# Two channel blocks taken last in the projection, and the modulation's strips multiplied by twos

## What is computed

```python
sh, sc, gt = adaln(c, w_ada, b_ada)              # silu(c) @ w_ada + b_ada, in three parts
sh_c, sc_c, gt_c = adaln(c_ctx[None], w_ada, b_ada)
h_l = rmsnorm(x_l, norm_g) * (1.0 + sc) + sh     # 512 x 2048
h_c = rmsnorm(x_c, norm_g) * (1.0 + sc_c) + sh_c # 256 x 2048
u_l = h_l @ w_in                                  # 2048 x 4928
u_c = h_c @ w_in[:, OFF_KV:OFF_MLA_G]
```

## Time and profile before

| what | value |
|---|---|
| median of 3 runs | 901.35 us |
| profiled execution | 901.99 us |
| its span | 900.2 us |
| mean granted TensorE clock | 0.997 |
| phase A on TensorE ends, phase B begins | 126.7 us |
| TensorE busy | 886.3 us, 98% |
| DMA | 184 MB, of it some 45 MB in the first 112 us |

### The profile page before, as it was taken

How to read it: one execution, slowest core, us unless ns; L and a number is a source line. 1 busy time by engine, 2 the same in 40 slices (tenths; PEclk the granted TensorE clock), 3 DMA queues, 4 the chain that set the end, 5 groups by cost and what they waited for, 6 DMA issues and landing times.

```text
span 900.2 us, 12252 instructions
## 1 busy us (share of the span) xinstructions
PE 886.3 (98%) x4750; PEld 739.2 (82%) x4750; DVE 696.5 (77%) x860; ACT 426.2 (47%) x633; POOL 200.0 (22%) x167
## 2 busy tenths in 40 slices
PE   9999999999999999999999999999999999999996
PEld 5776688888888888888888888989898988888885
DVE  5555898789997699967787484778687787879796
ACT  4655467434335434333324332645454456645464
POOL 1222200310003100001002753100000200495641
PEclk9999999999999999999999999999999999999998
DMA  9999932235473453578874242865657535875754
GB/s 362 417 420 421 409 145 95 89 129 189 143 183 106 114 167 117 187 232 325 314 295 162 94 140 94 181 228 141 135 171 198 123 140 187 305 228 187 234 186 187
DMA packets 36885, 184.08 MB, mean 204 GB/s; under 512 B 4411, under 2 KB 5819, under 8 KB 26716
## 3 DMA queue, kind: packets, MB, share of 16 engines
q1 hardware_dynamic: 32528, 147.25, 44.4%
q0 software_dynamic: 3968, 35.65, 16.2%
q10 hardware_dynamic: 332, 0.40, 0.1%
HBM read 177.39 MB, written 37.75 MB: 239 GB/s over the span
## 4 chain that ended last, share of the span: by engine, by line
PE 90%; DMA 4%; DVE 3%; ACT 2%; issue 1%; SPq 0%; ACTq 0%; DVEq 0%
PE pp L2346 41%; PE pp L2376 17%; PE pp L2656 17%; PE pp L2261 4%; DMA ada_raw<-in_w_ada_dram 3%; PE pp L2237 3%; PE pp L2622 2%; PE pp L2267 1%; PE pp L2613 1%; PE pp L2614 1%; DMA ada_raw<-in_w_scale_dram 1%; DVE softmax_stats L1854 1%; DVE pt_lo L1869 0%; ACT U L1140 0%; PE pp L2445 0%
## 5 line engine op out<-in xcount | busy, mean ns | idle before, releaser
L2346 PE MATMUL pp<-h_hi,w_hi 128*128 128x512 f32 x544 | 213.0, 391 | 0.0
L2346 PE MATMUL pp<-h_hi,w_lo 128*128 128x512 f32 x544 | 211.8, 389 | 0.0
L2346 PE MATMUL pp<-h_lo,w_hi 128*128 128x512 f32 x544 | 211.8, 389 | 0.0
L1569 DVE TENSOR_TENSOR w_lo<-w_raw,w_hi 128x1024 fp32r<-128x1024 f32 x68 | 91.0, 1339 | 62.6 <-ACT w_hi L931 61.8
L931 ACT ACTIVATE w_hi<-w_raw 128x1024 fp32r<-128x1024 f32 x68 | 71.8, 1056 | 130.8 <-PE pp L2346 114.9
L2346 PEld LDWEIGHTS pp<-h_hi,w_lo 128*128 128x128 f32 x544 | 102.1, 188 | 21.5
L2346 PEld LDWEIGHTS pp<-h_hi,w_hi 128*128 128x128 f32 x544 | 102.2, 188 | 21.1 <-DVE w_lo L1569 0.3
L2346 PEld LDWEIGHTS pp<-h_lo,w_hi 128*128 128x128 f32 x544 | 102.2, 188 | 20.5
L2656 PE MATMUL pp<-wo_hi,side_hi 128*128 128x512 f32 x224 | 87.3, 390 | 0.1
L2656 PE MATMUL pp<-wo_hi,side_lo 128*128 128x512 f32 x224 | 87.2, 389 | 0.0
L2656 PE MATMUL pp<-wo_lo,side_hi 128*128 128x512 f32 x224 | 87.2, 389 | 0.0
(11 more groups left out here) (368 smaller groups left out, 1930.8 us busy)
## 6 DMA issues: line engine op xcount, KB each, us to landing
w_raw<-in_wb_dram SPq DMA_DIRECT2D x68, 512.0 KB, 3.8
ada_raw<-in_w_ada_dram SPq DMA_DIRECT2D x15, 2048.0 KB, 13.5
w_out_sums<-in_w_out_dram POOLq DMA_DIRECT2D x16, 1024.0 KB, 10.4
w_gate_raw<-in_w_gate_dram SPq DMA_DIRECT2D x16, 1024.0 KB, 7.4
wo_raw<-w_out_sums SPq DMA_DIRECT2D x16, 1024.0 KB, 5.0
wo_raw<-in_w_out_dram SPq DMA_DIRECT2D x12, 1024.0 KB, 5.0
wa_raw<-in_wa_dram SPq DMA_DIRECT2D x14, 288.0 KB, 8.3
UG<-in_xT_dram SPq DMA_DIRECT2D x7, 512.0 KB, 9.2
```

Source lines behind the costliest of these rows:

```text
L1569: eng.tensor_tensor(lane(wb_lo, n % KW), lane(wb_raw, n % KW), lane(wb_hi, n % 2), ALU.subtract).then_inc(wb_lo_done, 1)
L2346: mm = eng.matmul(ps[i][:], w, x, start=(kk == 0 and m == 0), stop=(kk == KT - 1 and m == 2))
```

## The change

- Phase A's shifts for blocks 0 and 1 are no longer made in step 11. LATE is 16: the extra block is loaded after the others, multiplied in phase B's chunk 0, combined in chunk 1, and `shifted(0)` and `shifted(1)` run in chunk 2, on `wa` of blocks 0 and 1 loaded a second time. `wa_first` is gone.
- Phase B takes the channel blocks in the order 2, 3, ..., 15, 0, 1 (`place_of`, `block_at`; the host rolls `wb` to match), so the two blocks whose shift is late come last.
- `shift_columns` moves from phase A's last step to the end of chunk 3. The first two tiles are emptied without their shift, which `first_shifts` adds in chunk 4, with `centre` behind it (ScalarE's copy of the shift columns stands in its order for chunk 3, ahead of `evacuate(0)`); their neighbour taps move from chunk 2 to chunks 5 and 6.
- Of blocks 3 to 14, twelve blocks, two are multiplied one behind the other in every second step: 3 and 4 in step 2, 5 and 6 in step 4, and so on to 13 and 14 in step 12. Each pair has one copy of its rows, 512 columns wide. Block 15 stays in step 14, blocks 0, 1 and 2 where they were.

```diff
-NEIGHBOURS = (2, 2, 8, 8, 10, 10, 18, 19, 26, 26, 30, 34)
+NEIGHBOURS = (5, 6, 8, 8, 10, 10, 18, 19, 26, 26, 30, 34)
-EARLY, LATE = 2, 13
+EARLY, LATE = 2, KT
+STRIPS = {-1: (0,), 0: (1,), 1: (2,), 2: (3, 4), 4: (5, 6), 6: (7, 8), 8: (9, 10), 10: (11, 12), 12: (13, 14), 14: (15,)}
+def place_of(k):
+    return (k - EARLY) % KT
+def block_at(p):
+    return (p + EARLY) % KT
...
-        rows = at("mod_rows", TMP + 2.5, 256)
+        rows, late_rows = at("mod_rows", FREE + 25, 512), at("late_rows", TMP + 2.5, 256)
-        wa_first = at("wa_first", FREE + 25, EARLY * AW)
...
             for j in range(2, KT):
-                if j == LATE:
-                    load_ada(LATE)
-                load_ada(block_of(j))
+                load_ada(j)
...
+            load_ada(LATE)
             eng.wait_ge(ada_mm, KT - 1)
             for n in range(KW):
                 load_b(n)
             load_decay(0)
             load_decay(1)
+            load_wa(KT)
             eng.wait_ge(scaled, 4)
             load_w3(0)
             eng.wait_ge(a_lo_done, 2 * KT)
             eng.wait_ge(csum_done, KT)
+            load_wa(KT + 1)
...
+            def rows_out(j):
+                blocks = STRIPS[j]
+                eng.wait_ge(ada_mm, blocks[-1] + 1)
+                a = P if blocks[0] < EARLY else 0
+                eng.activation(rows[:, a:256 * len(blocks)], ps[7][:, a:256 * len(blocks)], ACT.Copy).then_inc(rows_done, 1)
...
             for j in range(KT - 1):
-                rows_out(block_of(j + 1))
+                if j in STRIPS:
+                    rows_out(j)
                 if j == 0:
                     rows_of_w(1)
-                modulation(j + 1)
+                for i, k in enumerate(STRIPS.get(j, ())):
+                    modulation(k, 4 * i, STRIPS[j][-1])
                 first_tokens(j + 1)
...
-                if j + 2 == LATE:
-                    rows_out(LATE)
-                    late_shifts()
...
+            def shift_columns():
+                eng.wait_ge(sum_mm, 4)
+                eng.activation(shift_cols[:], ps[7][:, 256:264], ACT.Copy).then_inc(root_done, 1)
+            def first_shifts():
+                eng.wait_ge(root_done, 4)
+                eng.wait_ge(evA_done, 5)
+                for i in range(2):
+                    eng.activation(conv_raw(i), conv_raw(i), ACT.Identity, bias=shift_cols[:, i:i + 1], scale=1.0).then_inc(shifted_in, 1)
+                for i in range(2):
+                    eng.wait_ge(shifted_in, 3 + i)
+                    centre(i)
...
             for i in range(2):
                 eng.wait_ge(a_scaled, i + 1)
-                eng.activation(conv_raw(i), ps[i][:], ACT.Identity, bias=shift_cols[:, i:i + 1], scale=1.0).then_inc(evA_done, 1)
+                eng.activation(conv_raw(i), ps[i][:], ACT.Copy).then_inc(evA_done, 1)
...
                 if n == 0:
-                    for k in range(8, 12):
-                        tokens(k)
+                    tokens(8)
+                    tokens(9)
+                    late_rows_out()
+                    hidden_high()
+                    tokens(10)
+                    tokens(11)
                 if n == 2:
+                    late_shifts()
                     tokens(14)
                     tokens(15)
...
+                if n == 3:
+                    shift_columns()
...
+                if n == 4:
+                    first_shifts()
...
-                if j + 2 == LATE:
-                    for k in range(EARLY):
-                        shifted(k)
...
                 if n == 2:
                     tokens(14)
                     tokens(15)
-                    for i in range(2):
-                        neighbour_taps(i)
+                    for k in range(EARLY):
+                        shifted(k)
...
-                    if i == 0 and j + 1 < KT:
-                        if j in (11, 12):
-                            eng.wait_ge(root_done, j - 10)
-                        ada_vectors(block_of(j + 1))
-                    if j + 2 == LATE and i == 3:
-                        eng.wait_ge(root_done, 2)
-                        ada_vectors(LATE)
+                    if i == 0:
+                        if j == 12:
+                            eng.wait_ge(root_done, 2)
+                        for x, b in enumerate(STRIPS.get(j, ())):
+                            ada_vectors(b, 256 * x)
+                    if i == 1 and j and j in STRIPS:
+                        combine(j)
...
                         if i == 1:
-                            shift_columns()
+                            context_square_sums()
...
                 half_chunk(n, 0)
+                if n == 0:
+                    ada_vectors(LATE)
...
                 half_chunk(n, 1)
+                if n == 1:
+                    combine_late()
+                if n == 3:
+                    shift_columns()
```

More of the change, by code:

```diff
@@ L836, in tokens, with late_rows_out @@
             def tokens(k):
-                if k >= KT - 2:
+                if k >= KT - EARLY:
                     eng.wait_ge(mmA_done, KT + 2)
+                    eng.wait_ge(mod_done, shifts_of(block_at(k)))
                 eng.wait_ge(scaled, k + 1)
-                s = k % 2
+                s, j = k % 2, block_at(k)
                 eng.activation(h_hi[:, bass.ts(k, L)], tmp[:, s * LK:s * LK + L], ACT.Identity,
[L842 to L847, removed]
+                               bias=mod[:, 4 * j:4 * j + 1], scale=1.0).then_inc(h_hi_done, 1)
+            def rows_out(j):
[3 more added lines that the diff above has]
+                eng.activation(rows[:, a:256 * len(blocks)], ps[7][:, a:256 * len(blocks)], ACT.Copy).then_inc(rows_done, 1)
+            def late_rows_out():
+                eng.wait_ge(ada_mm, LATE + 1)
+                eng.activation(late_rows[:], ps[7][:, 0:256], ACT.Copy).then_inc(rows_done, 1)
             def shift_of(k, at_column):
@@ L1233, in _ @@
                     tokens(13)
-                    eng.wait_ge(evA_done, 2)
-                    for i in range(2):
-                        centre(i)
-                if n == 0:
-                    hidden_high()
                 if n == 2:
+                    late_shifts()
                     tokens(14)
@@ L1449, in shifted @@
             def shifted(j):
-                w = wa_raw(j)
-                eng.wait_ge(wa_in[j % 2], 16 * (j // 2) + 16)
+                w, load = wa_raw(j), j + KT if j < EARLY else j
+                eng.wait_ge(wa_in[j % 2], 16 * (load // 2) + 16)
                 eng.wait_ge(mod_done, shifts_of(j))
@@ L2007, in _ @@
                 for i in range(12):
-                    if NEIGHBOURS[i] == n and n not in (2, 8, 18, 30, 34):
+                    if NEIGHBOURS[i] == n and n not in (5, 6, 8, 18, 30, 34):
                         neighbour_taps(i)
@@ L2039, in _ @@
                 for i in range(12):
-                    if NEIGHBOURS[i] == n and n in (18, 30, 34):
+                    if NEIGHBOURS[i] == n and n in (5, 6, 18, 30, 34):
                         neighbour_taps(i)
@@ L2240, in ada_vectors, with combined, combine, combine_late @@
                 mm.then_inc(ada_mm, 1)
-            def combine(b):
-                eng.wait_ge(rows_done, b + 1)
+            def combined(x, a, b, column):
                 if b >= EARLY:
-                    eng.matmul(ps[7][:, 0:2], rows[:, 0:P], comb[:], start=True, stop=True)
-                eng.matmul(ps[7][:, 2:4], rows[:, P:2 * P], comb[:], start=True, stop=True).then_inc(comb_mm, 1)
+                    eng.matmul(ps[7][:, column:column + 2], x[:, a:a + P], comb[:], start=True, stop=True)
+                eng.matmul(ps[7][:, column + 2:column + 4], x[:, a + P:a + 2 * P], comb[:], start=True, stop=True).then_inc(comb_mm, 1)
+            def combine(j):
+                eng.wait_ge(rows_done, sorted(STRIPS).index(j) + 1)
+                for i, b in enumerate(STRIPS[j]):
+                    combined(rows, 256 * i, b, 4 * i)
+            def combine_late():
+                eng.wait_ge(rows_done, len(STRIPS) + 1)
+                combined(late_rows, 0, LATE, 0)
             def tile(i, j):
@@ L2782, in layout @@
             + [tile(o_pool + i * P) for i in range(4)] + [tile(o_pg + i * P) for i in range(4)])
+    rest = [np.roll(x, -EARLY * P, axis=0) for x in rest]
     wa = np.concatenate(first, axis=1).reshape(KT, P, A_TILES * P - DR)
@@ L2786, in layout @@
     late = np.stack([w_ada[:, :P].reshape(KT, P, P), w_ada[:, P:2 * P].reshape(KT, P, P)], axis=2)[:, :, None]
-    blocks = np.concatenate([ss[:, :, EARLY:LATE], late, ss[:, :, LATE:]], axis=2)
+    blocks = np.concatenate([ss[:, :, EARLY:], late], axis=2)
     gate = w_ada[:, 2 * D:]
```

97 lines of the change are left out of this document (49 added, 48 removed).

## The result

The changed kernel takes 944.6 us (median of 5 runs, 941.26 to 945.15) against 901.35 (5 runs, 901.06 to 901.38): a ratio of 1.0474, with a 95% interval of [1.0456, 1.0492], as all intervals in brackets below. That is slower, as forecast, but by 43.2 us, twice the forecast 20.1 and outside its range.

The account below looks back on a forecast made before the run. TensorE was taken as the bound, with DMA able to rule in phase A. Phase B's delay 12.8, late block 2.5, shift products 1.7, chunk 4 wait 1.1 and ScalarE/VectorE 2.0 sum to 20.1 us: 921.5, range 917 to 926 (0.50).

Parts of the forecast that it names:

- S(2): Phase A: S(j) is the start of the tile behind step j's strips; for step 2 forecast at 34.8 us.
- the five cycles: Phase A, steps 2 to 12: two steps each, 17.15 us, or 15.9 without an x load, the queue running empty.
- S(14) to phase B: End of phase A, from the tile behind step 14's strips to phase B: unchanged at 10.4 us, bounds 8.7 and 10.4.
- The late strips: Phase B, chunks 0 and 1: the late block's strips and products moved from step 11 add 2.5 us.
- the wait ahead of chunk 4: Phase B: TensorE waits for ScalarE's shift copy and bank 0 copy, 1.1 us (0.3 to 2).
- not slower: DMA stays full: Rival, phase A: `wa` issued before the queue runs dry, so no change, 901 us; chance 0.04.
- the clock falls in the waits: Rival, phase A: new TensorE waits halve the clock, 2.9 us each fall; two or more, 926 to 939; chance 0.25.
- wa 0.7 + x 1.25 + block 5.0 + 2.4 from rest: Phase A, each two-step cycle: transfer times of the newly issued loads plus 2.4 us for starting an empty queue.
- the quiet chunk's row: Profile row: a 512 KB chunk on a quiet queue lands 3.6 us after issue, 1.25 transfer, giving 2.4 start delay.
- the queue recovers sooner: Rival, phase A: start delay and row-sum chain partly overlap, cycles lose 1.5 to 2 us each; 908 to 917, chance 0.17.
- S(12) to phase B: End of phase A: TensorE rules from 118.0, the tile start behind step 12's strips; phase B begins at 139.5 us.
- ScalarE and VectorE in chunks 4 on: Phase B, chunks 4 to 6: moved `first_shifts` and neighbour taps add 2.0 us; all hidden 0, all exposed 4.5.

Follow-up runs that it names:

- a third buffer: Third `wa` buffer, so `wa` waits one step further back: changed kernel, pairs kept, shift copy moved after `evacuate(0)`, 913.74 us; kernel before, 901.29 us.
- the fillers: Changed kernel with 8 to 20 small products in each pair, ahead of the wait for the second block: 936.58 us.
- singles: Changed kernel with one block of strips in each step instead of pairs: 909.19 us; with the shift copy also moved after `evacuate(0)`, 906.81 us.
- the copy behind: Changed kernel with ScalarE's copy of the shift columns after `evacuate(0)` instead of ahead of it in chunk 3: 942.7 us.
- the block ahead in the queue: Changed kernel, pairs kept, with SyncE issuing the `w_ada` block of step j+1 ahead of step j's `wa`: 916.59 us.

## Why the prediction was right about the sign and wrong about the size

**What held.** Block 4 holds up step 2 alone, and then every pair waits in its even step. S(2) to the issue of `wa` is 5.77 us (5.8). DMA starts from rest in each of the five cycles. Fewer changes of weights buy nothing: even with DMA full two steps take 13.7 to 14.1 us with a pair against 13.4. The shift products buy next to nothing in leaving phase A, and S(14) to phase B is 10.7 us (10.4). The late strips, the shift products and the wait ahead of chunk 4 put chunk 4 at 27.1 us of phase B against 22.1 before: 5.0, forecast 5.3. The rival "not slower: DMA stays full" is false for this kernel; the condition it names, a `wa` that goes out sooner, was made by a third buffer, and even then a loss of 1.6% is left: block 4's wait, the longer end of phase A, and the work in phase B do not go with it.

**Where the 22.5 us over the forecast's 20.1 came from** (42.6 in the spans), by the forecast's own steps:

- *The clock, 9.0 in six strips* (8.0 in the time, by the fillers). The forecast had none or one fall; the rest was the rival "the clock falls in the waits", priced at 2.9 for each of six falls and given a chance of 0.25. The rival's mechanism was right; holding it as a rival was the error. Its evidence was a 3.3 us idle stretch at the end of the kernel against 2.0 us in pieces; the six forecast waits of 3.0 to 4.2 us lay at the first, not the second, and this should have made it the forecast. Waits of 2.28 to 5.68 us were followed by the lower clock every time. The price was about twice too high (1.5 measured): a fall mostly covered the strips (+0.9 to +1.8) and hardly the tile. The Trainium skill, "TensorE: Matmul & The Clock Gate" (HAM oscillation), has this case, a wait for DMA in each tile that puts the clock back in each; the trace after agrees with it in six waits of six.
- *The term "wa 0.7 + x 1.25 + block 5.0 + 2.4 from rest", 5.9 over five cycles.* Mis-sized: the quiet chunk's row gave the delay before the first bytes, but the group also moves slowly in its first microseconds, and at 353 to 398 GB/s behind them, where the 5.0 for a block came from a queue at 415. 1.2 us more for each cycle, and 6.3 in all with the clock held by fillers. The rival "the queue recovers sooner" pointed the other way. The Trainium skill's fixed part of about 2.0 us for a transfer ("DMA: Bandwidth & Descriptors", the anatomy of a DMA, where it is stated for the SWDGE path) would have put the sum lower still; the landings decide against both.
- *S(12) to phase B, 24.8 us instead of 21.5.* The forecast let TensorE rule from S(12) on, with 11.1 us to S(14); it took 14.1. The chain after runs through VectorE: it makes two tokens' `h_lo` (2.44 us at 140.10) ahead of step 14's `a_lo` at 143.87, which TensorE waits for 1.75 us, and the tiles behind S(12) run partly at the lower clock. The `a_lo` wait stands also where the clock is whole (1.79 with fillers) and where DMA is full (1.78 with a third buffer), and not with singles. So pairs bring it; that they do so by making the steps uneven is our reading, not tried.
- *ScalarE and VectorE in chunks 4 on, 6.1 us instead of 2.0.* Two errors. Little of the moved operations is hidden: neighbour taps 1.6 and `first_shifts` 1.7 when cut to 16 columns, 3.3 of the 4.5 that the forecast had as "all exposed". And the clock's fall at 186.2 (1.6) was in no step: the forecast priced the wait in front of chunk 4 at 1.1, near the 1.0 measured, and did not ask what the clock makes of eight products with one column each and a wait behind them. These are 4.9 of the 6.1; the other 1.2, with the 0.66 us wait for the spectrum in it, stays without a trial.

S(12) is 15.4 late: 9.0 and 5.9, and 0.5 net in small pieces (`wa` issued up to 0.6 us later behind S(6), S(8) and S(10), the strips sooner behind each landing). With 3.3 behind it and 3.8 in phase B (6.1 less 2.0, less 0.3 in the terms ahead of chunk 4) this is the 22.5.

Divided by the experiments' times instead: of 43.2 us, pairs are 35.4, of which some 28 are the lead (and in them 8 the clock) and some 7 stay with any queue; the shift copy's place 2.4, the neighbour taps 1.6, `first_shifts` 1.7, the rest 2.1.

**What stays open.** Why phase A with pairs differs between executions (941.26 to 945.15 as changed, 937.63 to 945.57 with the copy behind). Why DMA stays under 415 GB/s in the five cycles after its slow start. How the 7 us that pairs cost with a third buffer divide between the wait at step 2 and the end of phase A is read off one profile, not tried.

## What to carry to other kernels

Where a queue feeds an engine that has no slack, multiplying two blocks in one step asks for one load a step earlier, and that lead must be there: count how many steps ahead each load can be asked for, before counting what the grouping saves. Price every new wait of TensorE twice, once for itself and once for the work that runs at 1.2 GHz behind it; in these profiles every wait of 2.28 us or more was followed by the lower clock, so here the second belonged in the forecast and not in a rival. A small copy put ahead of the one that frees a PSUM bank costs the wait that it makes (1.0 us here) and, right behind a run of one-column products, the clock as well (1.6).

## What the runs showed of the hardware that was not expected

- Eight fp32 products with one column (1.7 us, recorded as busy) and 0.84 us of idle time behind them were followed by the lower clock at 186.2; the same products with no idle time behind them were not (the copy behind `evacuate`). It was the same with singles: a fall at 150.1 behind 0.85 us of wait, none without. All four kernels profiled with the copy ahead of `evacuate` have this fall, and none of the five with it behind. In phase A before, waits of 0.54 to 0.86 us behind tiles of 512 columns left it at 1.00.
- A wait of 1.75 to 1.79 us for `a_lo` in step 14 came in all five kernels with pairs. It was followed by the lower clock in two (at 135.6 with fillers, at 115.8 with a third buffer) and not in the other three (as changed, with the block ahead in the queue, with the copy behind `evacuate`). So the length of a wait alone did not decide there.
- The lower clock can outlast its cause. In the profiled execution with pairs and the copy behind `evacuate`, it fell at 31.4 and came back at 45.1, though TensorE was busy without a gap for the last 9.8 us of that:

```profile
35.30:45.10 9.80, 9.80 (x38) 7.97 (x31) 2.67 (x5) 3.46 (x10) 0.00 (x0) 0.50 0.38 143
```

- Twenty filler products with 128 columns (forty instructions), 4.73 us in a wait that still left 1.02 us idle, kept the clock at 1.00.
- A queue that starts from rest with 0.3 MB, 0.5 MB and a 2 MB block moved 31, 257, 301 and 356 GB/s in its first four microseconds and 362 from there to the block's landing; a queue that was kept full moved 415.
